# A hybrid encoder layer: fourteen pairs of input tiles as two-by-two block products with seven multiplications, and the recurrent contraction moved to the end

## The chip, the cores and the metric

One core of one Trainium2 chip runs the whole layer. The metric is the time of one execution on the device in microseconds (us). Before the change the median of three runs is 1077.1 us (1075.72 to 1077.69).

## The reference

The layer takes x (1024 positions by 1024 features, float32). One input projection makes 56 column tiles of 128: q, k, v and a gate for attention, x and a gate for the ten blocks of a recurrent branch, and two merge gates for each of the eight output tiles.

```python
proj = einsum('bsd,de->bse', x, w_in) + b_in
q, k, v, g_attn, x_rnn, g_rnn, m_attn, m_rnn = split(proj, ...)
attn = window_attention(rope(q), rope(k), v, sink) * silu(g_attn)       # |i-j| <= 128
xc = centred_depthwise_conv(x_rnn, conv_w, conv_b)                      # width 4
rnn = bidirectional_rglru(xc, wa, ba, wx, bx, lam) * silu(g_rnn)        # 10 blocks of 128
merged = sigmoid(m_attn) * (attn @ w_branch_attn) + sigmoid(m_rnn) * (rnn @ w_branch_rnn)
x = layernorm(alpha * x + merged @ w_out + b_out, ln_gain, ln_bias)
```

For a recurrent block, two 128x128 matrices per direction make the gates r and i from xc; then a = exp(-8 r softplus(-lam)), u = sqrt(1 - a^2) i xc, and h[t] = a[t] h[t-1] + u[t] is scanned forward and backward and the two are summed.

## The kernel before

Features lie on the 128 partitions and positions along the free dimension. Every float32 operand is kept as a high and a low part (`_hi`, `_lo`), and a product is three matmuls: high by high, high by low, low by high (`half_products`). A unit is the weights of one column tile, 128x1024. It is loaded into `raw` by the queue of SyncE (SP), split by GpSimd (POOL) into `w_hi` and `w_lo` (a ring of two slots; `split`, called by `ring`), and multiplied with `xt_hi`, `xt_lo` by TensorE (PE) in `tile`: 8 contraction steps, 2 halves of 512 positions, 3 matmuls, so 48 matmuls of 128x512. The result lies in `buf[0]` or `buf[1]` (`proj` in the profile), two PSUM banks each; two more pairs of banks are `aux`. The semaphore `unit_split` counts units that are split, `filled` and `freed` count fills of a bank pair.

There are four stretches. First come the attention heads, which interleave small matmuls with the slices of the next tiles (to about 405 us). Then come ten recurrent blocks, b = 0 to 9. On PE a block is `gates(b, 0)` (12 matmuls into `aux`), a part of a branch projection, `gates(b, 1)` (12), the rest of that projection, the gate tile g of b and the x tile of b+2. For b = 0, 1 the projection is the attention branch, whose result ScalarE (ACT) copies to `part` and stores in DRAM (`spill`); for b from 2 it multiplies the earlier pair of blocks (`h_hi`, `h_lo`) by its weights, and VectorE (DVE) adds the partial result to `racc`. The third stretch makes the merge gates: eight pairs of tiles with a sigmoid on ACT and a multiply with `racc` and the reloaded attention branch on DVE (`merge`, loops over `TILES_C`), with the output weights split in between. The last one is the output projection, row block by row block (`rows_slice`, 384 matmuls), with the layer norm behind it.

Every engine works through its instructions in the written order, and waits at each until its semaphores are there. For one block ACT does, in this order: `pad_x` (evacuates x), `sigmoids(b, 0)` from `aux`, `conv_begin`, `sigmoids(b, 1)`, `decay_tanh`, `conv_high`, `decay_exp`, two `decay_square`, two `roots`, the sigmoid of `silu_gate`, and the copy of the state in `finish_block`. DVE does `gated_input` (`state<-state,conv`), three `conv_tap`, `conv_low`, two `one_less_decay`, `scan_input` (`state<-state,root`), two `scans`, `gated_sum`, and the `racc` adds between them. `gates(b, 1)` writes the same `aux` banks as `gates(b, 0)` and waits for `gate_freed`, that is for `sigmoids(b, 0)`.

## Time and profile before

| what | value |
|---|---|
| median of three runs | 1077.1 us |
| the profiled execution, its own time | 1080.0 us |
| its span, first to last instruction | 1078.2 us |
| granted TensorE clock, mean | 0.995 |
| busy: PE, DVE, ACT, POOL | 1053.1, 678.9, 397.1, 393.2 us |
| matmuls recorded | 4810 |

Times are from one profiled execution. A matmul's duration in the profile (0.39 us for 512 columns) overlaps with its neighbours'; what a matmul costs is the distance from start to start. A busy PE is therefore not a PE at its peak, and a count of matmuls in a stretch says more.

### The profile page before, as it was taken

What the parts mean: (1) busy time and instruction counts of PE and PEld (TensorE: products, weight loads), DVE (VectorE), ACT (ScalarE), POOL (GpSimd) and SP (SyncE); (2) the same over time, 40 slices, a digit from 0 to 9 for tenths busy, and PEclk for the clock granted to TensorE, in tenths of its full rate; (3) what the DMA queues carried; (4) which work ended last, traced back from release to release, by engine and by line L of the source; (5) the groups of instructions that cost most, each with busy time, mean ns of one, the idle gap of its engine ahead of it and who ended that gap; (6) DMA issues with size and microseconds to landing.
All of it is one profiled execution on the core that took longest, in us unless ns stands there. A gap on an engine that the chain in (4) does not pass through costs nothing.

```text
span 1078.2 us, 12849 instructions
## 1 busy us (share of the span) xinstructions
PE 1053.1 (98%) x4810; PEld 871.0 (81%) x4810; DVE 678.9 (63%) x797; ACT 397.1 (37%) x526; POOL 393.2 (36%) x199
## 2 busy tenths in 40 slices
PE   8999999999999999999999999999999999999996
PEld 6888788888887888878888888888888877888885
DVE  4767877106777754746887887878666333344565
ACT  3133333212334337456466456556520111111012
POOL 3421221332212134453553554355332445435123
PEclk9999999999999999999999999999999999999999
DMA  7210101241010111321211221111031233223412
GB/s 286 58 40 20 39 19 40 98 151 45 20 39 19 30 59 60 127 101 37 59 49 30 68 59 31 48 59 49 20 118 64 99 111 117 78 104 132 174 47 111
DMA packets 22668, 78.56 MB, mean 73 GB/s; under 512 B 2528, under 2 KB 2912, under 8 KB 22496
## 3 DMA queue, kind: packets, MB, share of 16 engines
q1 hardware_dynamic: 20032, 69.48, 19.6%
q10 hardware_dynamic: 2592, 8.48, 2.0%
q8 instruction: 30, 0.49, 0.2%
q14 instruction: 14, 0.11, 0.0%
HBM read 65.36 MB, written 12.58 MB: 72 GB/s over the span
## 4 chain that ended last, share of the span: by engine, by line
PE 85%; DVE 5%; issue 4%; DMA 3%; ACT 1%; POOL 1%; SPq 0%; DVEq 0%; ACTq 0%; POOLq 0%
PE proj L525 22%; PE proj L527 22%; PE proj L526 22%; PE aux L589 2%; DMA raw<-stream 2%; PE aux L526 2%; PE aux L525 2%; PE aux L527 2%; PE aux L571 2%; PE proj L758 1%; PE proj L757 1%; PE aux L758 1%; PE aux L757 1%; PE proj L756 1%; PE aux L756 1%
## 5 line engine op out<-in xcount | busy, mean ns | idle before, releaser
L525 PE MATMUL proj<-xt_hi,w_hi 128*128 128x512 f32 x896 | 357.7, 399 | 5.8 <-POOL w_lo L457 3.8
L527 PE MATMUL proj<-xt_hi,w_lo 128*128 128x512 f32 x896 | 351.1, 392 | 0.0
L526 PE MATMUL proj<-xt_lo,w_hi 128*128 128x512 f32 x896 | 350.8, 392 | 0.0
L454 POOL TENSOR_SCALAR w_hi<-raw 128x1024 fp32r<-128x1024 f32 (+1 forms) x74 | 93.6, 1264 | 576.8 <-PE proj L525 547.7
L457 POOL TENSOR_TENSOR w_lo<-raw,w_hi 128x1024 fp32r<-128x1024 f32 (+1 forms) x74 | 215.8, 2917 | 6.2
L525 PEld LDWEIGHTS proj<-xt_hi,w_hi 128*128 128x128 f32 x896 | 169.2, 189 | 39.2 <-issue 6.4
L527 PEld LDWEIGHTS proj<-xt_hi,w_lo 128*128 128x128 f32 x896 | 169.1, 189 | 36.8
L526 PEld LDWEIGHTS proj<-xt_lo,w_hi 128*128 128x128 f32 x896 | 169.5, 189 | 30.6
L839 ACT ACTIVATE probs<-masked,neg_max 128x385 f32<-128x385 f32 (+1 forms) x64 | 37.9, 592 | 135.9 <-DVE neg_max L1122 135.9
L1044 DVE TENSOR_TENSOR gate_r<-gate_r,racc 128x1024 f32<-128x1024 f32 x8 | 14.7, 1833 | 83.1 <-ACT gate_r L1014 83.1
L527 PE MATMUL proj<-h_hi,w_lo 128*128 128x512 f32 x160 | 62.6, 391 | 0.0
L525 PE MATMUL proj<-h_hi,w_hi 128*128 128x512 f32 x160 | 62.6, 391 | 0.0
L526 PE MATMUL proj<-h_lo,w_hi 128*128 128x512 f32 x160 | 62.6, 391 | 0.0
L1133 DVE TENSOR_SCALAR probs<-probs,rdenom 128x384 f32<-128x384 f32 (+1 forms) x64 | 54.9, 858 | 2.2
L1044 DVE TENSOR_TENSOR racc<-proj,racc 128x1024 f32<-128x1024 f32 x32 | 39.0, 1218 | 26.1 <-PE proj L527 26.1
L1044 DVE TENSOR_TENSOR state<-state,conv 128x1024 f32<-128x1024 f32 x20 | 33.1, 1657 | 33.3 <-ACT state L921 32.6
L1267 DVE TENSOR_TENSOR_SCAN state<-decay,state 128x1024 f32<-128x1024 f32 x20 | 51.9, 2632 | 0.0
L525 PE MATMUL proj<-at_hi,w_hi 128*128 128x512 f32 x128 | 49.9, 390 | 0.2 <-issue 0.2
L527 PE MATMUL proj<-at_hi,w_lo 128*128 128x512 f32 x128 | 49.8, 389 | 0.0
L526 PE MATMUL proj<-at_lo,w_hi 128*128 128x512 f32 x128 | 49.8, 389 | 0.0
L1047 DVE SCALAR_TENSOR_TENSOR rot_a<-proj,par,rotary 128x1024 f32<-128x1024 f32 x10 | 12.7, 1272 | 58.8 <-PE proj L527 58.8
L1047 DVE SCALAR_TENSOR_TENSOR root<-square,root 128x1024 f32<-128x1024 f32 x20 | 37.2, 1859 | 19.3 <-ACT square L944 18.8
(140 smaller groups left out, 1711.6 us busy)
## 6 DMA issues: line engine op xcount, KB each, us to landing
raw<-stream SPq DMA_DIRECT2D x80, 512.0 KB, 3.5
spill<-part ACTq DMA_DIRECT2D x16, 512.0 KB, 2.6
attn_in<-spill SPq DMA_DIRECT2D x8, 1024.0 KB, 5.0
x_raw<-x_t SPq DMA_DIRECT2D x8, 512.0 KB, 9.9
rows<-x_rows SPq DMA_DIRECT2D x8, 512.0 KB, 7.4
out<-rows SPq DMA_DIRECT2D x7, 512.0 KB, 2.6
raw<-stream SPq DMA_DIRECT2D x10, 256.0 KB, 2.7
rotary<-tables SPq DMA_DIRECT2D x1, 1024.0 KB, 12.3
```

The costliest lines, as they stand in the source:

```text
L454: nc.gpsimd.tensor_scalar(hi, raw[:, raw_slot, cols], 1.0, 0.0, ALU.mult, ALU.add)\
L457: nc.gpsimd.tensor_tensor(lo, raw[:, raw_slot, cols], hi.bitcast(f32), ALU.subtract)\
L525: begun = nc.tensor.matmul(bank, wh, mov_hi, start=first, stop=False)
L526: nc.tensor.matmul(bank, wh, mov_lo, start=False, stop=False)
L527: return begun, nc.tensor.matmul(bank, wl, mov_hi, start=False, stop=last)
L571: last = nc.tensor.transpose(pt_ps[:, i * P:(i + 1) * P], probs[:, n % 2, at:at + P], ident)
L589: last = nc.tensor.matmul(ot_ps[:, a * P:(z + 1) * P], v[:, kb * P:(kb + 1) * P], p[:, slot:slot + z - a + 1, :].rearrange("p n c -> p (n ...
L839: nc.scalar.activation(probs[:, n % 2, c0:3 * P + 1], masked[:, c0:3 * P + 1], ACT.Exp, scale=-1.0, bias=neg_max[:, 0:1], accum_out=denom[ ...
L1044: return nc.vector.tensor_tensor(dst, a, b, op)
L1047: return nc.vector.scalar_tensor_tensor(dst, a, scalar, b, op0, op1)
L1133: nc.vector.tensor_scalar(probs[:, n % 2, c0:3 * P], probs[:, n % 2, c0:3 * P], rdenom[:, 0:1], None, ALU.mult).then_inc(probs_ready, 1)
L1267: last = nc.vector.tensor_tensor_scan(state[d][:, ::turn], decay[d][:, ::turn], state[d][:, ::turn], 0.0, ALU.mult, ALU.add)
```

## The change

Fourteen pairs of input tiles (x of b+2 with g of b for b = 3 to 7, g9 with g8, and the two merge gates of each of the eight output tiles) are no longer made one by one. The pair's weights (2 column tiles) and x are each seen as a two-by-two block matrix: two halves of the contraction by two tiles, and two halves of the contraction by two halves of the positions. Seven block products of 12 matmuls (4 contraction steps, 3 matmuls) replace eight. In the code such a pair is a twin, and `twin_product(q, i)` is its product i.

- The four sums of weight blocks of each twin are made by POOL during attention (`presum_step`: four 512-wide operations a twin), stored in DRAM (`sums`) and loaded again as if they were weights.
- The sums of blocks of x (`t1`, `t2`, `t4` from a reloaded x, `t3` in place of a block of `xt`) are made by DVE, with high parts by ACT, in blocks 1 and 2 (`t_sums`, `t_low`, `t3_sums`, `t3_low`, `t_high`, `t3_high`).
- Weights come in halves of 512 columns with a ring of four slots. For three of seven products ACT makes the high part (`high_weights`) and POOL the low part; for four POOL makes both.
- The products accumulate in four single banks, and the order of use asks for copies between them: ACT copies a bank four times a twin (`early_copy`, `early<-proj`), DVE adds the copies to the banks (`twin_sum`, four 512-wide operations).
- The merge gates go through ACT's sigmoid to DRAM (`merge_gate`, `merges<-stage_out`) and come back at the end.
- The states of the recurrent blocks are stored in DRAM (`store_state`), loaded again (`load_h`), split (`h_high`, `h_low`), and contracted at the end in ten units (`BRANCH`) into all eight banks; the third stretch and `racc` are gone.

```diff
+NAMES_D = BRANCH[:6] + (("wo", 0), BRANCH[6], ("wo", 1), BRANCH[7], ...)
+PLAIN = 3
@@ sync (SP)
+            for t in range(4):
+                load_h(t, t // 2)
+            sp.wait_ge(product_split, PRODUCTS)
+            load_unit(NAMES_D[0])
+            load_unit(NAMES_D[1])
+            for t, product in ((4, 3), (5, 3), (6, 4), (7, 4), (8, 4), (9, 4)):
+                load_h(t, product)          # waits state_stored, 16 * (t + 1)
+            for n in range(2, 6):
+                load_parts(2 * n - 4)       # 4 DMAs of 512 KB each; from d = 2 on
+                load_parts(2 * n - 3)       # waits parts_gated, d - 1
+                load_unit(NAMES_D[n])
@@ tensor (PE)
+            def twin_product(q, i):
+                a, b, c, d = twin_banks(q)
+                before = 4 * (q - 1)
+                if i == 0:      # if q: wait twin_done, before + 1
+                    product(q, i, a, b11, True)
+                if i == 1:      # if q: twin_done, before + 2; else freed[0], t_split
+                    product(q, i, c, t1, True)
+                if i == 2:      # if q: early_done, before + 4
+                    product(q, i, b, b21, True)
+                if i == 3:      # early_done, 4 * q + 1
+                    product(q, i, a, t2, False)
+                if i == 4:      # if q: twin_done, before + 4
+                    product(q, i, d, t4, True)
+                if i == 5:      # early_done, 4 * q + 2
+                    product(q, i, c, b22, False)
+                if i == 6:      # early_done, 4 * q + 3; if q == 0: t3_split, 2
+                    product(q, i, a, t3, False)
...
             for b in range(RNN_BLOCKS):
                 gates(b, 0)
+                if b < 2:
+                    branch(b, 0)
+                if b >= PLAIN:
+                    twin_product(merge_of(b) if twin_of(b) is None else twin_of(b), 0)
                 gates(b, 1)
...
+                if b in (1, 2):
+                    rnn_tile(("g", b), 1)
+                if b < PLAIN:
+                    rnn_tile(("x", b + 2), 0)
+                if twin_of(b) is not None:
+                    for i in range(1, 7):
+                        twin_product(twin_of(b), i)
+                if b >= 2:
+                    for i in range(1 if b == RNN_BLOCKS - 1 else 0, 7):
+                        twin_product(merge_of(b), i)
@@ scalar (ACT), order in block b (q: its x, g twin; m: its merge twin)
+                if b >= PLAIN:
+                    early_copy(m', 3); merge_gate(m', 2); merge_gate(m', 3)   # m' of b-1
                 sigmoids(b, 0)
+                early_copy(q, 0); high_weights(q, 2)
                 conv_begin(b + 1); sigmoids(b, 1)
+                early_copy(q, 1)
                 decay_tanh(b)
+                if b == 2: t_high(2)
                 conv_high(b + 1); decay_exp(b)
+                early_copy(q, 2); high_weights(m, 0)
+                if b == 2: silu_gate(b)
                 decay_square(b, 0)
+                if b == 2: t_high(3); high_weights(m, 0)
+                high_weights(m, 1)
                 decay_square(b, 1)
+                early_copy(q, 3)
                 roots(b)
+                if b == 2: pad_x(b + 2); high_weights(m, 1)
+                early_copy(m, 0); high_weights(m, 2)
+                sigmoid_of(b); early_copy(m, 1)
+                if b == 2: t3_high(0); t3_high(1)
+                merge_gate(m, 0); early_copy(m, 2); high_weights(m + 1, 0)
+                store_state(b); merge_gate(m, 1); high_weights(m + 1, 1)
@@ vector (DVE), tail of block b
+                twin_sum(q, 2); twin_sum(q, 3)
                 scan_input(b)
+                silu_of(b)
+                if b == 2: t3_sums(0), t3_sums(1), t3_low(0), t3_low(1)
                 scans(b)
+                twin_sum(m, 0)
                 gated_sum(b)
+                twin_sum(m, 1)
```

The listing of ACT's and DVE's order above is condensed: one line for calls that stand one behind the other.

ACT's order in block 2, before, from the tanh of the decay to the padding of the next x (`h_hi` is the copy of the state, `silu_g` the gate):

```order
L929 ACTIVATE root<-decay,rate 128x1024 x2
L797 ACTIVATE conv_hi<-conv 128x1024
L936 ACT_TABLE_LOAD
L936 ACTIVATE decay<-decay,nrate 128x1024 x2
L944 ACTIVATE square<-decay 128x1024 x2
L950 ACT_TABLE_LOAD
L950 ACTIVATE root<-root 128x1024 x2
L904 ACT_TABLE_LOAD
L904 ACTIVATE silu_g<-proj,par 128x1024
L797 ACTIVATE h_hi<-state 128x1024
```

And now, from the second exponential to the first early copies of the first twin (`w_hi<-raw` is a high part of a product's weights):

```order
L1247 ACTIVATE silu_g<-proj,par 128x1024
L1289 ACTIVATE square<-decay 128x1024
L1137 ACTIVATE t_hi<-x_again 128x512 x3
L1137 ACTIVATE w_hi<-raw 128x512
L1289 ACTIVATE square<-decay 128x1024
L1295 ACT_TABLE_LOAD
L1295 ACTIVATE root<-root 128x1024 x2
L1226 ACTIVATE padded<-proj,par 128x1024
L1137 ACTIVATE w_hi<-raw 128x512
L1137 ACTIVATE early<-proj 128x512
```

The first weights of the first twin stand behind the sums of x, and the evacuation of the x tile behind the roots.

SP's order after the last product's weights, now (the state loads, the first two units of the contraction, the other state loads, the parts of two output tiles, the third unit):

```order
L610 DMA xf_lo<-states 128x2x512 x2
L610 DMA tf<-states 128x1024 x2
L503 DMA raw<-stream 128x1024 x2
L610 DMA tf<-states 128x1024 x4
L610 DMA xf_lo<-states 128x2x512 x2
L623 DMA xf_hi<-merges 128x2x512
L623 DMA xf_hi<-spill 128x2x512 x2
L624 DMA mf<-merges 128x1024
L623 DMA xf_lo<-merges 128x2x512
L623 DMA xf_lo<-spill 128x2x512 x2
L624 DMA mf<-merges 128x1024
L503 DMA raw<-stream 128x1024
```

Before, a loop in its place loaded two units and then the attention branch of one tile; now six state loads, the last of them of block 9, and eight loads of parts stand between the second and the third unit.

## Rows read from the trace of the kernel before

**Rows 1.** The page, busy time of the engines.
```profile
PE 1053.1 (98%) x4810; PEld 871.0 (81%) x4810; DVE 678.9 (63%) x797; ACT 397.1 (37%) x526; POOL 393.2 (36%) x199
```

**Rows 2.** Windows: stretch, its length, each engine's busy time (instructions), clock, DMA share, GB/s.
```profile
609.00:648.00 39.00, 39.00 (x172) 32.04 (x171) 32.25 (x21) 22.19 (x21) 18.49 (x8) 1.00 0.16 47
...
844.00:880.00 36.00, 34.01 (x143) 27.66 (x142) 17.40 (x10) 5.47 (x5) 18.97 (x10) 0.95 0.42 146
```

**Rows 3.** Timeline of PE in block 5: first matmul of a tile, and of the next.
```profile
625.85 0.39 PE L525 MATMUL proj<-xt_hi,w_hi 128*128 128x512 f32 x1
...
636.75 0.39 PE L525 MATMUL proj<-xt_hi,w_hi 128*128 128x512 f32 x1
```

**Rows 4.** Timeline of PE around a wait for weights in the merge stretch.
```profile
865.67 0.39 PE L527 MATMUL proj<-xt_hi,w_lo 128*128 128x512 f32 x1
868.05 0.49 PE L525 MATMUL proj<-xt_hi,w_hi 128*128 128x512 f32 x1 [1.99 <-POOL w_lo L457]
...
868.89 0.63 PE L525 MATMUL proj<-xt_hi,w_hi 128*128 128x512 f32 x1
869.32 0.63 PE L526 MATMUL proj<-xt_lo,w_hi 128*128 128x512 f32 x1
...
872.26 0.40 PE L527 MATMUL proj<-xt_hi,w_lo 128*128 128x512 f32 x1
```

**Rows 5.** Timeline of ACT in block 5.
```profile
610.83 1.12 ACT L921 ACTIVATE state<-aux,par 128x1024 f32<-128x1024 f32 x1 [0.22 <-PE aux L527]
...
621.22 1.06 ACT L797 ACTIVATE conv_hi<-conv 128x1024 fp32r<-128x1024 f32 x1 [0.36 <-DVE conv L1047]
622.29 1.28 ACT L936 ACT_TABLE_LOAD   x1
...
631.05 2.01 ACT L950 ACTIVATE root<-root 128x1024 f32<-128x1024 f32 x2
```

**Rows 6.** Timeline of ACT around a store in block 1.
```profile
455.94 0.34 ACTq L913 DMA_DIRECT2D spill<-part  x1
456.33 2.12 ACT L921 ACTIVATE decay<-aux,par 128x1024 f32<-128x1024 f32 x2 [0.42 <-ACT part L797]
```

**Rows 7.** Timeline of DVE, block 5, and one row of block 1.
```profile
616.57 4.62 DVE L1047 SCALAR_TENSOR_TENSOR conv<-padded,par,conv 128x1024 f32<-128x1024 f32 x3 [0.24 <-ACT conv L893]
...
632.22 3.51 DVE L1044 TENSOR_TENSOR state<-state,root 128x1024 f32<-128x1024 f32 x2 [0.28 <-ACT root L950]
635.65 5.26 DVE L1267 TENSOR_TENSOR_SCAN state<-decay,state 128x1024 f32<-128x1024 f32 x2
...
642.01 2.19 DVE L1044 TENSOR_TENSOR state<-state 128x1024 f32<-128x1024 f32 x1
...
470.86 2.36 DVE L1044 TENSOR_TENSOR state<-state,root 128x1024 f32<-128x1024 f32 x2 [1.22 <-ACT root L950]
```

**Rows 8.** Timeline of POOL: a half split in block 5, a whole one in the merge stretch.
```profile
632.50 2.14 POOL L457 TENSOR_TENSOR gates_lo<-raw,gates_hi 128x512 fp32r<-128x512 f32 x1
...
861.49 2.40 POOL L457 TENSOR_TENSOR wo_lo<-raw,wo_hi 128x1024 fp32r<-128x1024 f32 x1
```

**Rows 9.** Groups by form: operations of 512 elements (busy us, mean ns).
```profile
L1044 DVE TENSOR_TENSOR gated<-aux,gate 128x512 f32<-128x512 f32 x16 | 10.9, 684 | 0.0
...
L797 ACT ACTIVATE at_hi<-gated 128x512 f32 x12 | 7.5, 623 | 0.2
```

**Rows 10.** DMA issues (KB each, median us to landing), and a window of the start.
```profile
spill<-part ACTq DMA_DIRECT2D x16, 512.0 KB, 2.6
attn_in<-spill SPq DMA_DIRECT2D x8, 1024.0 KB, 5.0
...
16.00:20.00 4.00, 4.00 (x19) 3.34 (x18) 4.00 (x3) 3.36 (x4) 2.41 (x1) 1.00 1.02 414
```

**Rows 11.** Attention: DVE beside a POOL split, and the window of one stretch.
```profile
109.05 2.40 DVE L1133 TENSOR_SCALAR probs<-probs,rdenom 128x384 f32<-128x384 f32 x1
...
60.00:190.00 130.00, 126.07 (x654) 105.80 (x653) 97.24 (x204) 46.87 (x116) 25.75 (x14) 1.00 0.11 33
```

More of the change, by code:

```diff
@@ new lines, in columns_b @@
+    place(("merge", 0, 1))
+    place(("rnn", RNN_BLOCKS))
+    place(("rnn", RNN_BLOCKS + 1))
+    for first_d, count, _, before in TILES_C:
+        for d in range(first_d, first_d + count):
+            place(("merge", d, 0))
+            place(("merge", d, 1))
+        for n in (range(before, before + 2) if before < 4 else range(4, 8)):
+            place(("wo", n))
+    return found
+COLS = columns_b()
+NAMES_B = (("x", 1), ("gates", 0), ("attn", 0), ("attn", 1), ("x", 2),
+           ("gates", 1), ("attn", 2), ("attn", 3), ("g", 1), ("x", 3), ("gates", 2), ("g", 2), ("x", 4))
@@ new lines, in source, with branch_bank @@
+def source(n):
+    q, i = divmod(n, 7)
+    if ORDER[i]:
+        unit, half = ORDER[i]
+        return "stream", COLS[TWINS[q][unit]][0] + half * HALF
+    return "sums", (4 * q + SUM_AT[i]) * HALF
+PRESUMS = [[] for _ in range(UNIT_B)]
+_parts = [(q, part) for q in range(len(TWINS)) for part in range(2)]
+for _n, _part in enumerate(_parts):
+    PRESUMS[FIRST_PRESUM + _n * (UNIT_B - FIRST_PRESUM) // len(_parts)].append(_part)
+def branch_bank(b, t):
+    return t % 2 if b == 0 else 1 - t % 2
@@ L477, in _, with twin_weights @@
+            def twin_weights(q, gates_of):
+                for i in range(7):
+                    if ORDER[i]:
+                        own_weights(7 * q + i)
+                    else:
+                        sum_weights(7 * q + i)
+                    if i == 3 and gates_of:
+                        gate_weights_half(gates_of)
             for n in range(2):
@@ L1020, in _ @@
-            merge(0, 0)
-            for first_d, count, _, _ in TILES_C:
-                with act.Fori(0, count) as i:
-                    merge(i + first_d, i + (4 + first_d))
+                if last_one:
+                    merge_gate(m, 2)
+                    merge_gate(m, 3)
+                    h_high(2)
+                    h_high(3)
+                    sigmoid_of(b)
+                    store_state(b)
+                    for t in range(4, RNN_BLOCKS):
+                        h_high(t)
+                    break
@@ new lines, in _ @@
+                if m is not None:
+                    early_copy(m, 1)
+                    if b == 2:
+                        t3_high(0)
+                        t3_high(1)
+                    merge_gate(m, 0)
+                    early_copy(m, 2)
+                    high_weights(m + 1, 0)
+                    store_state(b)
+                    merge_gate(m, 1)
+                    high_weights(m + 1, 1)
+            for d in range(KT):
+                act.wait_ge(merged_done, d + 1)
+                copy(merged_hi[d][:, :], mf_lo[d][:, :]).then_inc(merged_hi_done, 1)
@@ L1342, in _, with gate_parts @@
-            merge(0, 0)
-            for first_d, count, _, _ in TILES_C:
-                with dve.Fori(0, count) as i:
-                    merge(i + first_d, i + (4 + first_d))
+                if b == 1:
+                    t_sums(0)
+                    t_sums(1)
+                    t_low(0)
+                    t_low(1)
+                if m is not None and not last_one:
+                    twin_sum(m, 1)
+            for t in range(4, RNN_BLOCKS):
+                h_low(t)
+            def gate_parts(d):
+                dve.wait_ge(parts_landed[d % 2], 64 * (d // 2 + 1))
+                gate, mine, other = parts(d)
+                tt(mine, mine, other, ALU.add).then_inc(parts_added, 1)
+                dve.wait_ge(parts_added, d + 1)
+                tt(two(mf_hi[d][:, :]), mine, gate, ALU.mult).then_inc(parts_gated, 1)
```

881 lines of the change are left out of this document (636 added, 245 removed).

## The prediction

> **What bounds the kernel now.** I read the page first: PE is busy for 1053.1 of 1078.2 us [rows 1], so TensorE sets the time, and the question of every other view is where it waits. The timeline of PE gives the price of a matmul: the 48 matmuls of one tile take 636.75 - 625.85 = 10.90 us, 0.227 us each [rows 3]. The windows show that the recurrent blocks run at that rate without a gap: 172 matmuls in 39 us at clock 1.00, while DVE is busy 32.3 us of the 39, ACT 22.2 and POOL 18.5 [rows 2]. In the merge stretch TensorE falls short: 36 us could hold 158.7 matmuls and hold 143, which is 3.6 us lost, beside reloads of weights [rows 2]; a second such place 48 us later costs about as much, so 7 us in all. There the timeline shows both halves of the price of a gap: from 865.67 to 868.05 nothing is issued, and then the distance is 0.43 us instead of 0.227 (1.2 GHz instead of 2.4) from 868.89 until 872.26 [rows 4]. 3.4 us at half rate cost 1.6 us on top of the gap.
>
> **What the change removes.** Each twin has 84 matmuls in place of 96, so 14 x 12 = 168 fewer: 168 x 0.227 = 38.1 us. The merge stretch and its two waits go: 7 us. Everything else of PE keeps its count, among it 480 matmuls of the recurrent contraction. Without any new wait the span would be 1078.2 - 38.1 - 7 = 1033.1 us. The `racc` adds on DVE vanish too; they were off the path.
>
> **What it adds, and where PE waits for it.** A product lasts 12 x 0.227 = 2.7 us, a twin 19.1, a block with its two twins and its gates 192 x 0.227 = 43.5. Banks and copies are needed one to three products later, and ACT and DVE work in a fixed order, so each wait of theirs can reach PE. Durations: sigmoid 1.12, copy 1.06, table load 1.28, two square roots 2.0 [rows 5]; 0.62 for a copy and 0.68 for an add of 512 [rows 9]; 0.42 of ACT's time for each store that it issues [rows 6]; three taps 4.6, scan input 3.5, two scans 5.3, state sum 2.2 [rows 7].
>
> Blocks 3 to 8. I lay one block out from its first gate matmul at 0. ACT begins with an early copy, two merge gates (0.68 + 0.42 each, and each behind a sum on DVE) and the sigmoids: the first sigmoid ends at 5.2 if ACT comes free at 0, and `gates(b, 1)` wants its bank at 5.4. The rest of ACT's list then runs: gates' second sigmoids until 12.3, tanh 15.1, conv copy 16.2, table and exponentials 19.6, early copy of the x, g twin at 20.2 (wanted 21.8, so in time), squares, the roots at 29.0. DVE follows: scan input until 31.9, `silu_of` 33.9 (behind a table load and a sigmoid on ACT until 32.6), scans 39.2, `twin_sum(m, 0)` 39.9, state sum and gating 43.3. `merge_gate(m, 0)` on ACT waits for that twin sum and ends at 41.1; the early copy queued behind it ends at 41.7 with the wake-up, and product 6 of the merge twin wants it at 40.8. So PE waits about 1.2 us. Behind that, `store_state` waits for the gating at 43.3, and ACT enters the next block 1.4 us late, which makes its first sigmoid 0.8 us late for `gates(b, 1)`. Together 2.1 us a block. From below: with DVE's two-input operations at their undisturbed speed (2.36 for the scan input instead of 3.51 [rows 7]) both waits nearly vanish, 0.3. From above: POOL has 14 low parts, 8 high parts and a gate split in each block, some 30 us of 43.5 instead of 18.5 of 39 [rows 2], and beside it DVE and POOL each slow down (3.51 against 2.36 for a pair [rows 7], 2.14 for half of what takes 2.40 whole [rows 8]); if all of the chain is met by it, 5 us. I take 2.3, near the walk whose rows come from the same blocks: 6 x 2.3 = 14 us, ends 2 and 30.
>
> Block 2 and the first twin. Block 1 ends on DVE with twelve operations of 512 for the sums of x, some 9 us, with six copies on ACT between; the sigmoids of block 2 stand behind them on ACT, and `gates(2, 1)` follows `gates(2, 0)` directly now: 2.3 us of wait. PE then runs g2 and x4 and wants the first product 21.8 us after `gates(2, 1)`. Its weights are behind, on ACT: conv copy, exponentials, a sigmoid with two table switches, a square, three copies that wait for DVE's third and fourth sums of x. They come 5.6 us late. Product 1 waits for x4's evacuation behind the roots: 1.2. Product 6 wants ACT's third early copy, which is queued behind `merge_gate(m, 0)`, which waits for `twin_sum(m, 0)`, which stands behind the scans, and these behind six subtractions and adds of 1024 (1.23 each undisturbed) and two more for t3: 6.6 us late. Sum 15.7 us, and the two gaps of over 2.4 us each cost the clock, 2 x 1.6. So 19 us, ends 14 and 24 (one clock loss and quick sums; all sums met by POOL).
>
> Block 9 into the contraction. 0.8 at the gates; then the first contraction unit waits for all twin sums, the last of which is behind ACT's squares and merge gates: 3.4, and a clock loss 1.6. Sum 5.8 us, ends 2 and 8.
>
> The third unit of the contraction is the largest single wait. SP must first load the state of block 9, which is stored some 49 us after that block began (the block's chain with merge gates and state copies put in), then issues eight loads of parts (4 MB) and only then the third unit. At 415 GB/s, the rate that the start reaches [rows 10], the 5.2 MB in the queue take 12.6 us; with the store's 2.6 us [rows 10] and a split of 3.5 us (2.40 for the low part [rows 8]) the unit is ready at 67.7. PE is done with two units at 52.1. Wait 15.6, clock 1.6: 17 us, ends 12 and 22 for a chain 5 us shorter or longer. Later units have 10.9 us each and 4.5 MB, 11.4 us, and stay just ahead because each is asked for a unit early.
>
> The output projection waits some 1.3 us for its seventh slice (bounds 0 and 3). In attention the 56 added POOL operations, about 1.2 us each, meet DVE: a scaling of 384 took 2.40 us beside a split [rows 11]. DVE has a fourth of its time free there (97 of 130 us busy [rows 11]), so I take 3 us, ends 0 and 10.
>
> **Sum.** 1033.1 + 14 + 19 + 5.8 + 17 + 1.3 + 3 = 1093.2 us of span. The profiled execution took 1080.0 with a span of 1078.2, and the median of the runs shown is 1077.1, 1.1 below that span; so 1092 us. The added waits, 60 us, are more than the 45 us removed. All low ends together give 1033 + 30, so 1062; all high ends 1033 + 97, so 1130, which takes every chain at its worst at once.
>
> **Rivals.**
> *Faster.* DVE's operations meet POOL less than before, because POOL's pieces are half as long. What speaks for it: an undisturbed pair is 1.15 us shorter [rows 7]. Then blocks 3 to 8 wait 2 us instead of 14, the first twin 14 instead of 19, the tail chains give back 4 at the third unit and 3 before it: 24 less, and with attention free 27, so 1065. It decides once the new waits stay under 45 us. Against it: POOL's total work grows. Chance 0.30, in which I count that I have walked a queue too strictly.
> *The clock falls in every block.* If the two waits of a block grow past 2.4 us together with the slow-down above, each takes 1.6 us more, up to 12 times: +19, so 1111. Against it, attention with its many small gaps keeps clock 1.00 [rows 11]. Chance 0.12. The Trainium skill has a rule that speaks for this rival (TensorE: Matmul & The Clock Gate, section on the second HAM failure mode): a TensorE that idles briefly between groups as it cycles through PSUM banks can swing between its two clocks. The products here cycle through four banks in just this way; the trace of before has no such cycling.
> *POOL becomes the bound.* A twin needs seven low and four high parts. At 2.14 us for a low half throughout [rows 8], 14 of them with 8 high parts and the gates make about 40 us of 43.5, and a piece that waits for ACT's part delays those behind it: +2.5 a block, 1107. Chance 0.08. The Trainium skill (Trainium Architecture — The Big Picture, section What this means for kernel authors) calls the port pair of DVE and GpSimd an exclusive lock and not a split of bandwidth; by that rule each would add whole pieces to the other, and this rival would be likelier. The rows show both sides slowed by about the overlap.
>
> **How the numbers follow.** Forecast 0.50, at 1092, its own range 1078 to 1108. Measurements of this kernel differ by some 0.2%, 2 us. Faster is the first rival, 0.30; of the forecast's cases 0.05 fall within 0.2%; slower is the rest, 0.65. The range for 8 in 10 reaches from 1054, below the sum of low ends since a mis-walked queue could save the third unit's wait, to 1112.
>
> **What would show it.** Right: 4642 matmuls; block distance 45 to 46.5 us; a PE gap of 5 us or more before the first product, one near 6 before its seventh, and one of 15 us before the third contraction unit, each followed by half-rate matmuls. Wrong: block distance 43.5, or the third unit's load issued before block 9's state is stored.

## The result, and the profile after

The changed kernel takes 1143.2 us (1141.5 to 1145.8) beside 1077.4 us for the kernel before in the same rounds: ratio 1.061, 95% interval 1.058 to 1.064. The direction was as forecast, the size not: +66 us instead of +15, outside the range. The page of the profiled execution of the kernel after, slices and groups left out, is to be read beside [rows 1]:

```profile
span 1143.9 us, 12951 instructions
...
PE 1055.2 (92%) x4642; PEld 847.0 (74%) x4642; DVE 722.6 (63%) x845; ACT 454.1 (40%) x651; POOL 589.7 (52%) x353
...
DMA packets 63541, 150.50 MB, mean 132 GB/s; under 512 B 6784, under 2 KB 7168, under 8 KB 63360
```

168 matmuls are gone, as planned, and PE is busy 2 us longer: its modelled busy time holds matmuls at half rate, and something else that a page doesn't show. These are PE's largest waits of the whole run (engine, line, what was waited for: us in total, times, longest):

```profile
PE proj L804 <- POOL w_lo L667: 18.4, 4, 16.4
PE proj L991 <- ACT early L1137: 13.9, 7, 5.6
PE aux L804 <- ACT state L1264: 11.3, 7, 2.7
PE proj L991 <- POOL w_lo L699: 8.6, 8, 2.9
...
PE proj L804 <- DVE stage_out L1506: 5.4, 1, 5.4
PE proj L1097 <- DVE merged L1503: 3.7, 1, 3.7
PE aux L804 <- DVE mf L1503: 3.6, 2, 2.8
```

Most of them the prediction's walk had named, in its places. It hadn't named those for POOL's low parts later in the twins (most of the 8.6 us) nor those before the sixth contraction unit (`mf`). The timeline of PE at the seventh product of the first twin, where 6.6 us were forecast, and at the third contraction unit, 15.6:

```profile
571.18 0.79 PE L991 MATMUL proj<-xt_hi,w_hi 128*128 128x512 f32 x1 [5.59 <-ACT early L1137]
571.77 0.63 PE L995 MATMUL proj<-xt_lo,w_hi 128*128 128x512 f32 x1
572.20 0.63 PE L997 MATMUL proj<-xt_hi,w_lo 128*128 128x512 f32 x1
...
943.64 0.80 PE L804 MATMUL proj<-t_hi,w_hi 128*128 128x512 f32 x1 [16.44 <-POOL w_lo L667]
944.24 0.63 PE L805 MATMUL proj<-t_lo,w_hi 128*128 128x512 f32 x1
944.66 0.63 PE L806 MATMUL proj<-t_hi,w_lo 128*128 128x512 f32 x1
```

Behind both, matmuls start 0.43 us apart, the 1.2 GHz level of [rows 4]. SP's queue ahead of the third unit is as forecast too: the load of block 9's state holds it for 29 us, eight loads of parts follow, then the unit (`raw<-stream`):

```profile
892.27 29.22 SPq L610 DMA_DIRECT2D xf_lo<-states  x2
921.68 1.14 SPq L623 DMA_DIRECT2D xf_hi<-merges  x1
...
928.36 0.43 SPq L503 DMA_DIRECT2D raw<-stream  x1
```

The waits don't add up to the 66 us lost and the 45 us that the removed work should have given. So I cut the run at PE's first matmul of each stretch and take from each length its matmuls at 0.2268 us, the price of [rows 3]:

| stretch (first matmul to first matmul of the next) | matmuls | lost | forecast |
|---|---|---|---|
| attention, to 416.08 (406.79 before) | - | 9.3 | 3 |
| blocks 0 and 1, 416.08 to 505.71 | 384 | 2.5 | 0 |
| block 2 with the first twin, to 576.34 | 204 | 24.4 | 19 |
| blocks 3 to 8, to 870.08 | 1152 | 32.5 | 14 |
| block 9, to 902.34 | 108 | 7.8 | 5.8 |
| contraction, to 1042.37 | 480 | 31.2 | 17 |
| output rows, to 1135.07 | 384 | 5.6 | 1.3 |

The sum is 113.3 us on top of 1033.1, 1146.4, within 2.5 of the span. Two rows are far off: blocks 3 to 8, where no single wait is over 2.7 us, and the contraction. And there is a loss in stretches that wait for nothing. The timeline of PE in block 0, `gates(0, 1)` done, shows it. The starts are 0.23, 0.23 and 0.24 us apart; from 427.28 to 444.08, 72 matmuls take 16.80 us, 0.2333 each, where the kernel before has 0.227 [rows 3].

```profile
427.28 0.39 PE L804 MATMUL proj<-at_hi,w_hi 128*128 128x512 f32 x1
427.51 0.40 PE L805 MATMUL proj<-at_lo,w_hi 128*128 128x512 f32 x1
427.74 0.39 PE L806 MATMUL proj<-at_hi,w_lo 128*128 128x512 f32 x1
427.98 0.40 PE L804 MATMUL proj<-at_hi,w_hi 128*128 128x512 f32 x1
```

### The profile page after: what moved, and what is told of

Its sections match the earlier page's. It is cut to its first block and busy times, and to the rows that moved or that the text cites. A ratio compares the mean times of both kernels' runs of the same rounds, so it can differ in the third digit from the quotient of the medians.

```text
span 1143.9 us, 12951 instructions
## 1 busy us (share of the span) xinstructions
PE 1055.2 (92%) x4642; PEld 847.0 (74%) x4642; DVE 722.6 (63%) x845; ACT 454.1 (40%) x651; POOL 589.7 (52%) x353
## 5 line engine op out<-in xcount | busy, mean ns | idle before, releaser
L804 PE MATMUL proj<-xt_hi,w_hi 128*128 128x512 f32 x480 | 196.9, 410 | 9.4 <-DVE stage_out L1506 5.4
L805 PE MATMUL proj<-xt_lo,w_hi 128*128 128x512 f32 x480 | 190.5, 397 | 0.0
L806 PE MATMUL proj<-xt_hi,w_lo 128*128 128x512 f32 x480 | 190.4, 397 | 0.0
L699 POOL TENSOR_TENSOR w_lo<-raw,w_hi 128x512 fp32r<-128x512 f32 x66 | 117.4, 1785 | 47.7 <-ACT w_hi L1137 39.8
L667 POOL TENSOR_TENSOR w_lo<-raw,w_hi 128x1024 fp32r<-128x1024 f32 (+1 forms) x46 | 120.0, 2609 | 3.8
L991 PE MATMUL proj<-xt_hi,w_hi 128*128 128x512 f32 x224 | 91.3, 408 | 18.4 <-ACT early L1137 13.9
L806 PEld LDWEIGHTS proj<-xt_hi,w_lo 128*128 128x128 f32 x480 | 90.7, 189 | 22.0
L805 PEld LDWEIGHTS proj<-xt_lo,w_hi 128*128 128x128 f32 x480 | 91.0, 190 | 15.7
L995 PE MATMUL proj<-xt_lo,w_hi 128*128 128x512 f32 x224 | 90.0, 402 | 0.0
L997 PE MATMUL proj<-xt_hi,w_lo 128*128 128x512 f32 x224 | 89.9, 401 | 0.0
L991 PE MATMUL proj<-t_hi,w_hi 128*128 128x512 f32 x168 | 67.7, 403 | 4.1 <-POOL w_lo L699 4.1
L1506 DVE SCALAR_TENSOR_TENSOR conv<-padded,par,conv 128x1024 f32<-128x1024 f32 x30 | 55.2, 1841 | 25.3 <-ACT conv L1236 24.6
L995 PE MATMUL proj<-t_lo,w_hi 128*128 128x512 f32 x168 | 67.3, 400 | 0.0
L997 PE MATMUL proj<-t_hi,w_lo 128*128 128x512 f32 x168 | 67.0, 399 | 0.0
```

Source lines behind the costliest of these rows:

```text
L667: nc.gpsimd.tensor_tensor(lo, raw[:, raw_slot, cols], hi.bitcast(f32), ALU.subtract)\
L699: nc.gpsimd.tensor_tensor(lo, src, hi.bitcast(f32), ALU.subtract).then_inc(product_split, 1)
L804: begun = nc.tensor.matmul(bank, wh, mov_hi, start=first, stop=False)
L805: nc.tensor.matmul(bank, wh, mov_lo, start=False, stop=False)
L806: return begun, nc.tensor.matmul(bank, wl, mov_hi, start=False, stop=last)
L991: first = nc.tensor.matmul(bank, wh[:, c], moving[0][:, k, :], start=opens and k == 0, stop=False, skip_group_check=True)
```

## The experiments

### Why a matmul costs 0.2333 us now

The change moves three small tensors (`stats`, `moments`, `norm`) out of the region ahead of x. In the compiled kernels the weights `w_hi` start at byte 24704 of each partition in both, `xt_hi` at 47232 before and at 46656 after. Over a multiple of 256 that is 128 for the weights, 128 for x before, 64 after. There are two theories: the place of the two operands in their partitions, or the traffic of POOL and DMA, which do 1.5 and 1.9 times the work. Two kernels test them with an unused tensor, `filler`, that pushes x along: one puts the places right in the kernel after, the other puts them wrong in the kernel before.

```diff
 # a_place64 (after)                      # b_place128 (before)
-        allot(ctx, "filler", [P, 22])     -        allot(ctx, "filler", [P, 24])
+        allot(ctx, "filler", [P, 38])     +        allot(ctx, "filler", [P, 56])
```

> The changed kernel with its filler 16 floats longer, so that xt_hi, xt_lo and everything behind them lie 64 bytes higher; nothing else is touched. In the trace of the changed kernel a 512-column matmul follows the last after 0.233 us, before the change after 0.227. Theory (place): the distance depends on where the moving operand starts relative to the stationary one. Before the change x and weights both start 128 bytes above a multiple of 256 and run at 0.227, and the second h slot, at 0, runs at 0.233; after it the weights are at 128 and x at 64. With x at 128 again the distance goes back to 0.227 in nearly all matmuls: 4000 x 0.0065 = 26 us less, so 1117 us, and the same waits. Rival (traffic): POOL and DMA, both much busier than before, slow TensorE's reads; the distance stays 0.233 and the time 1143.

> The kernel before with its filler 32 floats longer, so that xt_hi, xt_lo and everything behind them lie 128 bytes higher; weights stay. Theory (place): x, at and conv are then at 0 above a multiple of 256 and the weights at 128: 0.233 us from matmul to matmul, while the second h slot comes to 128 and runs at 0.227. Some 3500 matmuls of 512 columns lose 0.0065 us, 22 us: 1099 us, with POOL and DMA doing exactly what they did. Rival (traffic): nothing changes, 1077.

Measured: a_place64 1138.2 us (ratio to before 1.057, 1.055 to 1.060), b_place128 1090.2 (1.013, 1.011 to 1.015). The timelines of PE show, in the first, 72 matmuls of block 0 from 423.98 to 440.30, 0.2267 each. In the second, the 96 of two x tiles from 593.17 to 615.56 take 0.2332 each, and ahead of them 36 that read the second of two buffers of the states (the second h slot), from 585.00, take 0.2269. In the kernel before it was the other way round: that slot ran at 0.233 and x at 0.227.

```profile
423.98 0.39 PE L804 MATMUL proj<-at_hi,w_hi 128*128 128x512 f32 x1
...
440.30 0.40 PE L804 MATMUL proj<-xt_hi,w_hi 128*128 128x512 f32 x1
```

```profile
585.00 0.39 PE L525 MATMUL proj<-h_hi,w_hi 128*128 128x512 f32 x1
...
593.17 0.40 PE L525 MATMUL proj<-xt_hi,w_hi 128*128 128x512 f32 x1
...
615.56 0.40 PE L525 MATMUL aux<-conv_hi,gates_hi 128*128 128x512 f32 x1
```

So it is the place: the price changed in each kernel for just those operands whose place changed, with traffic unchanged. The rule of the Trainium skill that a DMA never contends with a compute engine (SBUF — State Buffer, section Who interferes with whom) agrees: a_place64 moves as many bytes as the kernel after and is back at 0.2267. But both times missed: 5 us came back where I wrote 26, and 13 were lost where I wrote 22. Attention gave only 3.0 and 1.8 us of it (first gates at 413.10 instead of 416.08, at 408.61 instead of 406.79); that other engines set its pace is my reading, and no run tests it alone. In a_place64 the blocks stayed nearly as far apart as they were. Two more kernels, measured once each, bound the rule:

> The changed kernel with its filler 80 floats longer: x and what follows lie 320 bytes higher, so moving operands start 128 above a multiple of 256 like the weights, but 384 above a multiple of 512, where the weights are at 128. If equal places modulo 256 are enough, 0.227 us from matmul to matmul and 1138; if it takes 512, 0.233 and 1143.

> The changed kernel with its filler 24 floats longer: x and what follows lie 96 bytes higher, at 160 above a multiple of 256, 32 off the weights' 128. Differences of 64 and 128 gave 0.233. If any difference does, 0.233 and 1143; if one of 32 is as good as none, 0.227 and 1138.

Measured: 1138.3 with 132 matmuls of the first two tiles at 0.2277, and 1144.8 with 128 at 0.2341; the first 96 of block 0 run at 0.2267 and 0.2333. So equal places modulo 256 are enough, and a difference of 32 bytes is as slow as one of 64 or 128.

### What the sums of weights cost in attention

```diff
-                    nc.gpsimd.tensor_tensor(b, a, b, ALU.add).then_inc(presummed, 1)
-                    nc.gpsimd.tensor_tensor(a, c, a, ALU.subtract).then_inc(presummed, 1)
...
+                    pool.sem_inc(presummed, 3)
```

> The changed kernel without the 56 additions and subtractions of weight blocks that POOL makes during attention; their loads and stores stay, so the stored sums are plain weight blocks and the output is another. In the trace block 0 begins 9.3 us later than before the change (416.1 against 406.8). Theory (POOL meets DVE there): of the 9.3 some 6 to 7 is the longer distance of matmuls and 3 is these operations, so block 0 begins near 413 and the time is 3 us less, 1140. Rival (POOL costs most of it): block 0 begins at 408 to 410, 1136. Rival (the loads and stores cost it): no change, 1143.

Measured: 1135.7 us, 7.5 less; block 0 begins at 409.57 instead of 416.08. The windows of attention, kernel after and then a_nosum (busy time and instructions of PE, PEld, DVE, ACT, POOL, then clock, DMA share, GB/s):

```profile
60.00:190.00 130.00, 125.42 (x644) 103.96 (x643) 96.57 (x198) 47.34 (x116) 54.06 (x35) 1.00 0.33 110
```

```profile
60.00:190.00 130.00, 126.58 (x653) 105.82 (x652) 97.15 (x203) 46.94 (x117) 25.87 (x15) 1.00 0.30 101
```

With 28 us more of POOL, 9 matmuls and 5 operations of DVE fewer fit into 130 us. The rival that POOL costs most of it holds: 6.5 us by this pair, 3.0 by the place, for the 9.3 of the table. Neither share is sharp: among the later kernels with the sums and the operands in place, block 0 begins between 411.3 and 414.8. The loads and stores cost nothing that shows: s_nosum (below) does them all, has the operands in place, and begins block 0 at 405.26, ahead of the kernel before.

### What sets the distance of the blocks

ACT's first sigmoid of a block, in blocks 4 and 5 of the kernel after, then of a_place64 (timelines of ACT):

```profile
629.25 2.12 ACT L1264 ACTIVATE state<-aux,par 128x1024 f32<-128x1024 f32 x2 [0.46 <-ACT stage_out L1339]
...
677.84 2.12 ACT L1264 ACTIVATE state<-aux,par 128x1024 f32<-128x1024 f32 x2 [0.46 <-ACT stage_out L1339]
```

```profile
625.01 2.12 ACT L1264 ACTIVATE state<-aux,par 128x1024 f32<-128x1024 f32 x2 [0.46 <-ACT stage_out L1339]
...
673.51 2.12 ACT L1264 ACTIVATE state<-aux,par 128x1024 f32<-128x1024 f32 x2 [0.46 <-ACT stage_out L1339]
```

The sigmoids are 48.6 and 48.5 us apart. In a_place64 a block's 192 matmuls are 1.3 us shorter and the block isn't: TensorE's own work doesn't set the distance. ACT of the kernel after just ahead of 629.25 (each merge gate waits for DVE):

```profile
624.52 0.58 ACT L1137 ACTIVATE early<-proj 128x512 f32<-128x512 f32 x1
625.98 0.63 ACT L1339 ACTIVATE stage_out<-stage_out 128x512 f32<-128x512 f32 x1 [0.88 <-DVE stage_out L1506]
...
628.16 0.63 ACT L1339 ACTIVATE stage_out<-stage_out 128x512 f32<-128x512 f32 x1 [1.55 <-DVE stage_out L1506]
```

and DVE there, whose sum waits for the earlier result's store:

```profile
625.19 0.75 DVE L1506 SCALAR_TENSOR_TENSOR stage_out<-early,par 128x512 f32<-128x512 f32 x1 [2.33 <-issue]
627.38 0.75 DVE L1506 SCALAR_TENSOR_TENSOR stage_out<-proj,par,early 128x512 f32<-128x512 f32 x1 [1.43 <-DMA merges<-stage_out]
```

The last scan of a block, its state sum, `twin_sum`, `merge_gate`, their stores and two more of each stand ahead of the next block's sigmoids, and from those sigmoids the next scans follow. So the chain closes on itself; I call it a ring, and its length is the least distance of two blocks. p_act takes the last two merge gates out of it, and moves one early copy ahead of merge gate 0. Like all kernels below except a_tail it has the operands in place.

```diff
                 if b >= PLAIN:
                     early_copy(m', 3)
-                    merge_gate(m', 2); merge_gate(m', 3)
                 sigmoids(b, 0)
+                if b >= PLAIN:
+                    merge_gate(m', 2); merge_gate(m', 3)
...
+                    early_copy(m, 2)
                     merge_gate(m, 0)
-                    early_copy(m, 2)
```

> The changed kernel with the operands back in place (filler 16 floats longer) and ACT's order in the blocks changed at two points: the merge gates 2 and 3 of the earlier block's twin come behind the first two sigmoids instead of ahead of them, and the third early copy of the merge twin ahead of merge gate 0. Putting the operands back alone made each matmul 0.0065 us shorter, and yet blocks 3 to 8 stayed 48.5 us apart, so TensorE doesn't set that distance. Theory (ring through ACT): from the first sigmoids of a block over gating, taps, decay, roots, scans and state sum to the merge gates with their stores and on to the next first sigmoids takes 48.5 us; without the last two merge gates in it the ring is 4 us shorter, and a block takes about 44.5, near TensorE's own 43.5: 6 x 4 = 24 us less, and 4 more at the first twin's seventh product, so 1110 beside 1138 for the operands alone. Rival (walk of step 1: two separate waits of 1.4 and 1.3 us): 6 x 2.7 = 16 us less, 1122. Rival (POOL's weights, busy 38 of 48.5 us): the waits move to POOL, at most 1 us a block is won, 1132.

Measured: 1112.9 us (1.033, 1.030 to 1.036), 25.3 less than a_place64. The sigmoids stand at 616.90 and 662.00, 45.1 apart:

```profile
616.90 2.12 ACT L1264 ACTIVATE state<-aux,par 128x1024 f32<-128x1024 f32 x2
...
662.00 2.12 ACT L1264 ACTIVATE state<-aux,par 128x1024 f32<-128x1024 f32 x2
```

This bears out the ring: PE's first matmuls of blocks 4 to 8 are 45.1 us apart, and in a_place64 48.4 to 48.5. That gives 3.4 us a block, where the rival of two separate waits has 2.7. The total alone wouldn't decide. In the two profiles blocks 3 to 8 together give 17.4 us, near the rival's 16, since block 3 got longer; block 2 gives 7.9, where the wait before the first twin's seventh product, 5.6 us, became 1.4 by the early copy that moved. How the 3.4 us divide between the two moves wasn't tried. For the 1.6 us that are left over 43.5 there are two edits: q_all (below) lets ACT make the next twin's weights ahead of merge gate 0, and r_pool takes two pieces a block from POOL.

> The seven edits that ran at 1103.7, and the high part of product 5's weights of every twin made by ACT (behind its second early copy) instead of POOL. In that run moving ACT's other weights ahead didn't shorten a block (45.1 us again): POOL is busy without a pause from 638 to 661 us there and the waits of 1.1 and 0.25 us in each block are for its low parts. Theory (POOL is the limit at the end of a block): two pieces of 1.1 to 2.6 us less per block, the distance goes from 45.1 to 43.7, and 6 x 1.3 = 8 us less, 1096. Rival (the ring through ACT, now with 1.2 us more in it, binds again): 45 or more, 1104 to 1106.

Measured: 1104.2 us, against 1103.7 without it, with the sigmoids at 612.25 and 657.33, 45.1 apart again. POOL's low parts in the kernel after, 640 to 675 us (shortest, median, longest in ns), show why POOL looked like the limit:

```profile
L699 POOL TENSOR_TENSOR w_lo<-raw,w_hi x8: 1293/2207/3137, 638.6 to 673.8; 128x512 fp32r<-128x512 f32 x8
```

But less work for it gave nothing. The rival's number came out; whether the ring binds again or POOL's pieces, stretched by DVE's scans, fill what they are given, these runs don't tell apart.

### Block 2, and the contraction

> As the run before with the reordered ACT, and in block 2 the high part of the first product's weights is made ahead of the sigmoid of the gate tile instead of behind four squares and copies. Theory: the wait before the first product, 2.7 us and half-rate matmuls behind it, goes, about 4 us less than that run, 1106. Rival (POOL's low part or the second sums of x are late next): nothing is won, 1110.

The edit moves `high_weights(m, 0)` ahead of `silu_gate(2)`. Measured: 1111.5, 1.3 less than p_act, which is not clear of the spread (1108.7 to 1112.4 against 1110.9 to 1115.5). PE no longer waits before the first product and waits 4.4 us before the second, for the evacuation of x4. Nothing is won, as the rival has it, but what is late next is neither of the two that it named.

a_tail loads each contraction unit ahead of its parts, and the state of block 9 behind the third unit:

```diff
             for n in range(2, 6):
+                load_unit(NAMES_D[n])
+                if n == 2:
+                    load_h(9, 4)
                 load_parts(2 * n - 4)
                 load_parts(2 * n - 3)
-                load_unit(NAMES_D[n])
```

> The changed kernel with SP's order changed at the contraction alone: the third unit is loaded ahead of the state of block 9 and of the first eight parts, and each later unit ahead of its parts. Theory (queue): the third unit's wait of 16.4 us and the half-rate matmuls behind it go, about 18 us: 1125, unless the parts, now later, hold up the merges. Rival (the parts are late next): the merges free the banks 5 to 10 us later and TensorE waits there instead, 1130 to 1135. Rival (POOL's split is what is late): the wait stays, 1143.

Measured: 1141.8, 1.4 less than the kernel after, which is within the spread. The 16.4 us are gone and have come back in two places, as PE's waits in a_tail show, the first before the sixth unit and the second, of 5.1 us, before the fourth:

```profile
PE proj L806 <- DVE mf L1505: 10.1, 1, 10.1
...
PE proj L806 <- POOL w_lo L669: 6.0, 3, 5.1
```

The sixth unit (`mf`) needs banks that the merges free, and DVE merges only after it has gated all eight sets of parts. The last of these are issued until 968 and are there at 975.8:

```profile
975.80 1.22 DVE L1505 TENSOR_TENSOR xf_lo<-xf_lo 128x1024 f32<-128x1024 f32 x1 [2.83 <-DMA mf<-merges]
```

> The changed kernel with the operands back in place, and SP's order at the contraction changed: third unit, the first eight parts, and then the state of block 9; DVE gates the first two pairs of parts before it splits that state. Moving the unit alone took the 16.4 us wait away and gave 10.1 + 5.1 us back at the sixth unit and the fourth, where banks wait for all parts to be gated: 16.8 MB of parts took the DMA from 922 to 968. Theory (parts bind): with 4 MB of them on the way before the state of block 9 is stored, they end 10 us sooner and neither wait is left: 15 us less than the operands alone, 1123. Rival (DVE, which has block 9's scans to do, gates the parts no earlier): 3 to 5 us less, 1134.

Measured: 1132.8, 5.4 less than a_place64: far from 15, and just above the rival's 3 to 5.

> Operands in place, ACT's order, block 2's weights and the order at the contraction together. Theory: the gains add, 28 + 4 + 15 from 1138, so 1091, and the change still doesn't pay, since the four added stretches (first twin, ring of a block, contraction without its parts, slower attention) eat the 38 us of 168 matmuls. Rival: with the blocks at TensorE's pace the tail has nothing to wait for, and it comes under the kernel before, 1070.

Measured: 1105.9. The three gains add (25.3 + 1.3 + 5.4 = 32.0 of 32.3), within a spread of some us (1102.3 to 1109.2). A wait of 11.4 us now stands before the fourth unit.

> The four edits together, which ran at 1105.9, with three more moves. (1) In block 2 the evacuation of x4 and the next weights ahead of the roots: that run's first-product wait had moved to product 1, 4.4 us behind this evacuation, with half-rate matmuls after it; theory -6. (2) ACT makes the first weights of the next twin ahead of merge gate 0 instead of behind it: in that run each block waited 1.1 + 0.25 us for POOL's low part of these, which waits for ACT's high part; theory -1.2 a block, -7. (3) SP loads the fourth unit too ahead of the state of block 9, the fifth and sixth behind the third and fifth set of parts: the 11.4 us wait of that run was for the fourth unit, issued at 898.5 behind 4 MB of parts; theory -12. Sum 1081. Rival: what is late next takes half of it, as in each step so far, 1093.

Measured: 1103.7 instead of 1081: none of its three moves did what I wrote. PE waits as long before product 1 (4.3 us), now for the last sums of x, whose low parts DVE ends at 539.6. The block distance is the same. The fourth unit is in time, and PE waits 12.7 us before the sixth:

```profile
940.01 0.76 PE L809 MATMUL proj<-xt_hi,w_hi 128*128 128x512 f32 x1 [12.73 <-DVE mf L1509]
```

> As the run before, and without POOL's 56 sums of weight blocks in attention (loads and stores stay; the stored sums are plain weight blocks, so the output is another). In the changed kernel leaving them out brought block 0 forward by 6.5 us and the time down by 7.5. Theory: the same here, 6.5 us less than the run before, about 1074 to 1086. Rival: with the blocks no longer bound by their ring it makes no odds elsewhere, or DVE is the limit of attention anyway, 0 to 2 us.

Measured: 1095.9, 7.8 less than q_all.

> The seven edits, and DVE's order at the contraction changed: it gates the first two sets of parts ahead of the last three states but one, and does the first four merges, which free the banks, ahead of the last two sets. In the run with seven edits TensorE waits 12.7 us before the sixth unit, since the first merge stands behind all eight sets, whose 16.8 MB arrive until 937 us. Theory: the first merge follows the sixth set, at 929, and the sixth unit starts 8 to 10 us sooner: 1094. Rival (the output weights or the splits that POOL makes are late next): 2 us less, 1102.

Measured: 1101.6. The first merge is early enough, and the wait, 12.4 us, stands before the seventh unit, as the rival has it. POOL in r_tail sits idle for 23.6 us in `output_weights(0)`, which waits for all parts to be gated, and the seventh unit's split is behind it:

```profile
944.08 1.04 POOL L696 TENSOR_SCALAR xt_hi<-raw 128x1024 fp32r<-128x1024 f32 x1 [23.59 <-DVE mf L1509]
...
947.52 1.04 POOL L669 TENSOR_SCALAR w_hi<-raw 128x1024 fp32r<-128x1024 f32 x1
```

> Both edits of the two runs before on top of the seven. Theory: the gains add, 1103.7 - 8 - 10 = 1086; still slower than the kernel before by 0.7%. Rival: one of them fails, 1095.

> As the run before, without POOL's 56 sums of weight blocks in attention (stored sums are plain weight blocks, so the output is another): what the change could reach if these sums cost nothing. Theory: 7.5 us less, 1078, as fast as the kernel before within 0.5%: the 168 matmuls' 38 us are then just paid for by what is left in block 2, before the contraction and in it. Rival: 1088.

Measured: 1102.4 and 1091.9; the wait at the seventh unit is in both. The last two kernels have the order of r_tail with the seventh and eighth unit ahead of the output weights, in the list that SP and POOL share:

```diff
-NAMES_D = BRANCH[:6] + (("wo", 0), BRANCH[6], ("wo", 1), BRANCH[7], ("wo", 2), BRANCH[8], ("wo", 3),
-                        BRANCH[9], ("wo", 4), ...
+NAMES_D = BRANCH[:8] + (("wo", 0), BRANCH[8], ("wo", 1), BRANCH[9], ("wo", 2), ("wo", 3),
+                        ("wo", 4), ...
```

> The seven edits with DVE's new order at the contraction, which ran at 1101.6, and the eighth and seventh weight units ahead of the first piece of the output weights in SP's and POOL's order (output weights 0 behind the eighth unit). In that run the wait left the sixth unit and came back before the seventh, 12.4 us on POOL's low part: POOL's split for it stands behind output weights 0, which wait until all eight sets of parts are gated. Theory: nothing of this wait is left, the clock stays up, 12 us less, 1090. Rival: the banks, freed by merges behind the parts, are late next and half is given back, 1096.

> As the run before, without POOL's 56 sums of weight blocks in attention (the stored sums are plain weight blocks, so the output is another). Theory: 8 us less, as twice before, 1082, still 0.5% slower than the kernel before. Rival: 1077 or less, the change would pay if the sums were free.

Measured: s_all 1089.9 (1.012, 1.009 to 1.015), s_nosum 1079.0 (1.003, 1.001 to 1.004). The list of PE's waits in s_all has little of the contraction left but its start:

```profile
PE proj L996 <- POOL w_lo L704: 13.0, 10, 2.9
...
PE proj L809 <- DVE stage_out L1512: 6.7, 1, 6.7
PE proj L996 <- issue: 5.2, 1, 5.2
...
PE proj L1102 <- DVE merged L1509: 3.9, 1, 3.9
```

s_all is the best version that computes the layer (s_nosum leaves out the sums of weights), 53 us under the changed kernel and 13 over the kernel before. Without the sums the four pairs gain 7.5, 7.8, 10.4 and 10.9 us; no run shows why it becomes more.

## Why the prediction was right or wrong

**What holds.** The removed part: 4642 matmuls, and no cost in them. The direction, by the argument of the sum: waits of engines in a fixed order cost more than 168 matmuls are worth. The places: 2.3 forecast and 2.30 measured at `gates(2, 1)`, 5.6 and 2.7 before the first product, 1.2 and 0.4 at product 1, 6.6 and 5.6 at product 6, 3.4 and 5.4 before the contraction, 15.6 and 16.4 at its third unit, and half-rate matmuls behind the long ones.

**"Everything else of PE keeps its count"** was true, and was read as if it kept its price too. So the step "Without any new wait the span would be 1078.2 - 38.1 - 7 = 1033.1 us" failed. Nearly all matmuls up to the output rows cost 0.0066 us more by the place of x. The rows of the kernel before held the clue, since its second h slot ran at 0.233 (36 matmuls from 579.05 to 587.44) and I looked at one tile [rows 3]. Its worth was small in this kernel, 5 us, because the blocks were bound elsewhere, and 13 in the kernel before.

**Blocks 3 to 8, 32.5 us instead of 14.** The step that failed is "if ACT comes free at 0": I laid one block out from its start and took two lags of 1.2 and 0.8 us, instead of following ACT from a block's sigmoids to the next's. The end of the walk, "ACT enters the next block 1.4 us late", was not fed back. The ring is 48.5 us; the waits that PE shows (1.4 and 1.3 us, and 0.3 for a low part) are only what 192 matmuls leave of it. The walk's 43.5 + 2.1 us were 3 too few ("block distance 45 to 46.5 us"); with two merge gates and an early copy moved it is 45.1. Block 8 took 52.5: its wait at `gates(8, 1)` was 2.7 us, with half-rate matmuls behind it.

**The contraction, 31.2 instead of 17.** The wait at the third unit came out (16.4 for 15.6, and 24 matmuls at 0.324 instead of 0.233 behind it, 2.2), in part by luck: PE was done with two units 57.1 us after block 9 began, not 52.1, and the third was ready at 73.6, not 67.7. "Later units stay just ahead" failed: three waits at the sixth unit (1.1 for its split, 2.8 and 0.8 for banks) cost 7.0 with their slow matmuls, because the banks hang on all eight sets of parts. The rest is place, 480 x 0.0066 = 3.2, and 2.3 of half rate at the first unit, which the forecast has in the term before. Four reorderings moved the wait to the fourth, sixth and seventh unit; only the fifth removed it.

**Attention, 9.3 instead of 3**, is still within the ends of 0 and 10. The cost of POOL's sums was mis-sized, 6.5 instead of 3, and DVE's free fourth didn't hide them; the rest is the place. **Block 2, 24.4 instead of 19**, is outside its ends by 0.4. That its waits sum to 15.1 for 15.7 is luck: 1.2 and 2.9 of it are for POOL's low parts at products 3 and 4, which the walk didn't have, and the wait before the first product was half of what it had. And four of them are long enough for half rate behind them, not two: 7.3 us for 3.2, and 204 x 0.0066 = 1.4 of place. **Block 9** (7.8, and 10.1 with the half rate behind it, for 5.8) and the **output rows** (5.6 for 1.3, a wait of 3.7 with half-rate matmuls behind it, bounds 0 and 3) were forecast too low as well.

**The rivals.** "Faster" was wrong. On the whole DVE and POOL meet more, not less: three taps take 6.2 us instead of 4.6 [rows 7] and two scans 5.9 instead of 5.3, though the first multiply of the gates takes 2.4 instead of 3.2. The fall of the clock in every block didn't come: waits of 1.3 to 1.4 us in each block left it at 1.00 in the window 629.0 to 677.6, and only block 8 with its 2.7 us had it. So the swing of the Trainium skill (TensorE: Matmul & The Clock Gate, section A second HAM failure mode) isn't shown here. Its time, 1111, would have been nearer, for another reason. POOL as the bound isn't borne out: p_act leaves POOL's work as it is and gains 3.4 us a block, and r_pool takes work from it and gains nothing. That the Trainium skill calls the port pair an exclusive lock (SBUF — State Buffer, Who interferes with whom) fits with a low part of 1.29 us that takes up to 3.14 beside DVE, and doesn't show whether DVE waited as long.

All of this together: from 1143.2, the place and ACT's order give 30.3 us, block 2 and the contraction with its orders 23.0, the sums 10.9 (if they were free): 1079.0. What s_nosum still loses over 1033 is in block 2 (18 us: one wait of 2.4 at its gates, one of 4.3 for the last sums of x, three for POOL's low parts, and half rate behind them), 1.6 us a block, and the start of the contraction (6.6) and of the output rows (3.9); none of these was tried further. (A slip without weight: the sum of all high ends is 1129 and not 1130, if 1.1 us go off it as off the low one.)

## What to carry to other kernels

When a change only removes work from the engine that is busiest, ask first how long the ring is: follow the in-order engines from one block's first instruction to the same one of the next, with everything that was added to their lists, and compare that length with the busiest engine's. A wait that is taken away by moving one transfer comes back at the next instruction that hangs on the same data, so price the data's arrival and not the wait. And measure the matmul's distance again after any change of the allocation, since a few bytes of filler decide 3% of it.

## What the runs showed of the hardware

- A float32 matmul of 128x512 starts 0.2266 to 0.2268 us after the last where moving and stationary operand start at the same place modulo 256 bytes in their partitions, and 0.233 where they differ by 32, 64 or 128 (six kernels, weights at 128). The common place itself doesn't matter as far as it was varied: in the output rows both operands lie at 64 (after), 128 (before), 160 (a_place96) or 0 (b_place128), and it is 0.2267 in all four.
- That price hardly shows in attention: b_place128 lost 1.8 us in 400 there.
- In the kernel after, waits of TensorE of up to 1.4 us were followed by matmuls at full clock, and those of 2.3, 2.7, 5.6 and 16.4 us by matmuls 0.43 us apart. In the kernel before, this came behind waits of 1.99 [rows 4] and of 1.84 us (at 915.33).
- In a window with 393 GB/s of DMA (940 to 960) matmuls at full clock (the 48 from 948.61) stay at 0.2333 us, the price of their place.
